# Expert outputs of a mixture of experts added straight into the output rows, with a weight ring of three

## The chip, the cores and the metric

The kernel runs on one core of one Trainium2 chip. A core has five engines with instruction streams of their own: TensorE (PE, matrix products; its weight loads are shown apart as PEld), VectorE (DVE), ScalarE (ACT), GpSimd (POOL) and SyncE (SP), which here only issues transfers. They wait for each other with semaphores. Sixteen DMA engines move data between the memory of the chip and the on-chip buffer; transfers are issued from SP, ACT (hardware queues) or POOL (the software queue, the one that does indirect transfers). Matrix products write to PSUM, and an engine copies the result out. The metric is the device time in microseconds of one execution, lower is better.

## The reference

One decoder layer for 512 prompt tokens and 8 sample tokens (520 rows of 1024 values, f32). The change lies in the last part, a mixture of experts in which each token goes to one group and inside it to two experts:

```python
def hier_moe(x, g_ffn, w_group, w_router, w_gate, w_up, w_down):
    h = rmsnorm(x, g_ffn).reshape(b * t, d)
    g_logits = jnp.dot(h, w_group)                      # 4 groups
    g_sel = jnp.argmax(g_logits, axis=-1)
    g_w = softmax(g_logits) at g_sel
    e_in_group = jnp.dot(h, w_router) of group g_sel    # 8 experts each
    top_val, top_idx = lax.top_k(e_in_group, 2)
    top_w = jax.nn.softmax(top_val, axis=-1) * g_w
    ...
    def add_expert(acc, params):
        wg, wu, wd, c = params                          # (1024,512) (1024,512) (512,1024)
        act = jax.nn.silu(h @ wg) * (h @ wu)
        return acc + (act @ wd) * c[:, None], None
y = x + hier_moe(x, ...)
```

There are 32 experts. Each has three weight matrices of 2 MB in f32, so all weights together are 192 MB, and every one of them is read.

## The kernel before

The layer up to the mixture (projections, two attentions, output projections) takes the first 794 us and is untouched but for one line of clearing. The rest has three blocks, one after the other. Between blocks all engines meet at a barrier.

**`route`** normalises the rows (`hn`, stored in device memory as `token_rows`), computes the router's products, and finds on VectorE, in a chain of small dependent operations, which expert each token goes to and at which place. Each expert has a block of `CAP` = 64 rows; a token beyond 64 would go to one of 16 extra blocks (`NX`), which are run in a loop of their own, as often as needed (here no such round shows in the trace). From the places a small product on TensorE (`TB`, ten products with the one-hot tables `Rk` and `Bk`) makes `table[row, block]`, the token number of each place, or a number out of range for an empty place. SP meanwhile issues the weights of experts 0 and 1 into the two places of the ring `ew`, and behind them the stores of `hn`.

**`experts`** goes through the 32 experts with two sets of buffers (`j` = expert mod 2): two experts written out, then a hardware loop of 15 rounds with two experts each. For one expert:

- POOL copies a column of `table` to `idx` and gathers the rows to `xg` (an indirect transfer; empty places move nothing).
- PE turns `xg` (eight transposes to `TX`), DVE scales it into `xT`, PE forms the gate product `G` and the up product `U`. The 64 token rows fill only half the columns of the array, so each product is made in two halves of the hidden values side by side: half `h` takes the weight columns `HW*h` to `HW*h+255` and writes PSUM rows `64*h` on.
- ACT takes the sigmoid of `G`, DVE multiplies into `a`, PE turns `a` (`AT`), DVE copies it to `aT`, PE forms the down product `Y`.
- ACT copies `Y` to `y` and issues two stores of 128 KB into `expert_rows` (`eout`), all 64 rows, filled or not.
- SP waits in turn for the gate, up and down product of expert e-2 and issues the weights of expert e to the freed place.

In memory the gate and up weights of one partition are 8 rows side by side, 16 KB in one piece; the down weights of one partition are four rows of 4 KB that lie 512 KB apart (`"(j p) c -> p j c"`).

**`combine_experts`** gathers for each tile of 128 tokens its two expert rows (`yg`), DVE multiplies them with the weights `wt` and adds them to the residual `x`, and SP stores the tile to the output.

## Time and profile before

| | |
|---|---|
| median of 3 runs | 1392.73 us (1385.19 to 1395.62) |
| the profiled execution, own time | 1395.67 us |
| its span | 1393.4 us |
| before `route` | 0 to 794 us |
| `route` | 794 to 856 us |
| `experts` | 857 to 1366 us |
| `combine_experts` | 1368 to 1393 us |
| PE busy, share of the span | 1139.0 us, 82% |
| DVE busy | 506.3 us, 36% |
| memory read and written by DMA | 283.76 MB and 21.24 MB |

Read it by stage. The share of a busy engine is an average over blocks with different limits, and the change touches the last 600 us, where the DMA engines, PE and chains of small operations take turns as the limit.

### The profile page before, as it was taken

The numbers are of one execution on the slowest core, as the hardware profiler recorded it, in microseconds if no ns is written. First come the engines' busy times: TensorE is split into PE (matmuls) and PEld (weight loads), VectorE is DVE, ScalarE is ACT, GpSimd is POOL, SyncE is SP. The second block draws the span as 40 slices with busy tenths as digits, with TensorE's granted clock in tenths as the row PEclk, the third lists the DMA queues.
The fourth block names the chain that finished last, engine by engine and source line by source line (L and its number), as shares of the span: only waits on it lengthen the run. The fifth ranks groups of instructions, "written<-read, shape, count | busy, mean of one in ns | idle before, by whom it ended". The sixth has DMA issues, their size and how long they took to land. (4 is left out here: it accounts for less than half of the span.)

```text
span 1393.4 us, 16542 instructions
## 1 busy us (share of the span) xinstructions
PE 1139.0 (82%) x6089; PEld 604.4 (43%) x6089; DVE 506.3 (36%) x1187; ACT 179.6 (13%) x429; POOL 116.4 (8%) x161
## 2 busy tenths in 40 slices
PE   4989998895988899979999865888787878777771
PEld 3634444343555544423345354454444434444440
DVE  3426958974555256742113153111111111111113
ACT  2102221102444101101010100000000000000000
POOL 2012102200000000000010101000000000000003
PEclk9999999995577699989999955999999999999996
DMA  6332102103000345563540190999999999999995
GB/s 205 106 133 83 61 31 84 68 31 125 1 1 1 121 136 196 183 239 121 181 148 5 40 387 11 399 412 410 418 414 413 409 419 416 416 415 414 414 394 193
DMA packets 82263, 301.56 MB, mean 216 GB/s; under 512 B 17868, under 2 KB 17868, under 8 KB 74020
## 3 DMA queue, kind: packets, MB, share of 16 engines
q1 hardware_dynamic: 69108, 267.20, 49.3%
q0 software_dynamic: 7984, 25.30, 5.1%
q10 hardware_dynamic: 5120, 8.39, 1.7%
q8 instruction: 29, 0.48, 0.1%
q14 instruction: 22, 0.18, 0.0%
HBM read 283.76 MB, written 21.24 MB: 219 GB/s over the span
## 5 line engine op out<-in xcount | busy, mean ns | idle before, releaser
L344 PE MATMUL p_z<-m_w,m_xT 128*128 128x512 f32 (+2 forms) x528 | 214.6, 563 | 7.2 <-DMA m_w<-in_w_in 6.6
L1582 PE MATMUL e_Y<-x_ew,e_aT 128*64 128x512 f32 x512 | 128.8, 648 | 39.5 <-issue 21.3
L344 PEld LDWEIGHTS p_z<-m_w,m_xT 128*128 128x128 f32 (+1 forms) x528 | 95.1, 194 | 114.8 <-issue 107.7
L1567 PE MATMUL e_G<-x_ew,e_xT 128*64 128x256 f32 x1024 | 119.2, 386 | 29.2 <-DVE e_xT L1604 29.2
L1567 PE MATMUL e_U<-x_ew,e_xT 128*64 128x256 f32 x1024 | 117.0, 381 | 17.1 <-DMA x_ew<-in_w_up 17.1
L967 PE MATMUL g_ring<-m_w,m_xT 128*128 128x512 f32 x256 | 118.0, 615 | 0.0
L1567 PEld LDWEIGHTS e_G<-x_ew,e_xT 128*64 128x64 f32 x1024 | 78.0, 138 | 60.3 <-issue 18.9
L1567 PEld LDWEIGHTS e_U<-x_ew,e_xT 128*64 128x64 f32 x1024 | 74.4, 137 | 57.0 <-DMA x_ew<-in_w_up 24.9
L1582 PEld LDWEIGHTS e_Y<-x_ew,e_aT 128*64 128x64 f32 x512 | 42.4, 147 | 105.2 <-issue 81.0
L1604 DVE TENSOR_TENSOR e_xT<-e_TX,x_gffn 128x512 f32<-128x512 f32 x32 | 22.1, 692 | 179.6 <-PE e_TX L1558 179.6
L967 PEld LDWEIGHTS g_ring<-m_w,m_xT 128*128 128x128 f32 x256 | 49.0, 197 | 63.3 <-issue 62.1
L1607 DVE TENSOR_TENSOR e_den<-e_sig,e_G 128x256 f32<-128x256 f32 x32 | 13.5, 421 | 138.4 <-ACT e_sig L1590 138.4
L1594 ACT COPY e_y<-e_Y 128x512 f32<-128x512 f32 x32 | 18.7, 585 | 321.0 <-PE e_Y L1582 321.0
L1612 DVE TENSOR_TENSOR e_a<-e_den,e_U 128x256 f32<-128x256 f32 x32 | 13.5, 421 | 106.6 <-PE e_U L1567 106.6
L724 ACT ACTIVATE a_prob<-a_masked,a_nb 128x128 f32<-128x128 f32 (+3 forms) x64 | 35.9, 561 | 78.4 <-DVE a_nb L806 78.2
L1182 DVE TENSOR_TENSOR g_prod<-g_page_k,g_B 128x512 f32<-128x512 f32 x64 | 41.0, 680 | 6.5 <-PE g_B L1004 4.0
L681 PE MATMUL a_S<-t_Tkd,t_Tqd 64*128 64x128 f32 (+3 forms) x64 | 30.8, 749 | 12.9 <-DVE a_nb L806 9.2
L1621 POOL COPY e_idx<-x_table 64x1 int32 (+1 forms) x32 | 5.7, 178 | 397.3 <-PE e_TX L1558 397.3
L660 PEld LDWEIGHTS a_O<-t_vvs,a_pT 128*128 128x128 f32 x160 | 34.3, 304 | 0.1
L461 POOL TENSOR_TENSOR p_rs<-p_rs,k_c 128x8 f32<-128x8 f32 (+1 forms) x20 | 33.6, 1680 | 1.7
L967 PE MATMUL g_ring<-g_wod,m_oTd 128*128 128x512 f32 x64 | 30.9, 628 | 3.4 <-DMA g_wos<-in_w_o_dsa 3.4
L660 PE MATMUL a_O<-t_vvs,a_pT 128*128 128x64 f32 x160 | 33.6, 369 | 0.0
(332 smaller groups left out, 1277.4 us busy)
## 6 DMA issues: line engine op xcount, KB each, us to landing
x_ew<-in_w_gate SPq DMA_DIRECT2D x32, 2048.0 KB, 26.9
x_ew<-in_w_up SPq DMA_DIRECT2D x32, 2048.0 KB
x_ew<-in_w_down SPq DMA_DIRECT2D x32, 2048.0 KB, 27.8
m_w<-in_w_in SPq DMA_DIRECT2D x9, 2048.0 KB, 7.7
g_page_k<-in_cache_diff_k SPq DMA_DIRECT2D x32, 256.0 KB, 2.7
g_page_k<-in_cache_dsa_k SPq DMA_DIRECT2D x32, 256.0 KB, 2.8
g_page_v<-in_cache_diff_v SPq DMA_DIRECT2D x32, 256.0 KB, 4.2
g_page_v<-in_cache_dsa_v SPq DMA_DIRECT2D x32, 256.0 KB, 3.1
```

The lines of the kernel that those rows point to most:

```text
L344: last = nc.tensor.matmul(z[u % 3][0:p, 0:WIDTH[k]], s.xT[:, j, 128 * i:128 * i + p], s.w[:, c % 2, j, 0:WIDTH[k]], start=j == 0, stop=j = ...
L461: nc.gpsimd.tensor_tensor(rs[0:p, n % 2, :], rs[0:p, n % 2, :], s.c[0:p, C_MH:C_MH + H], ALU.pow).then_inc(rs_ready, 1)
L660: last = nc.tensor.matmul(O[g % 2][:, w * h:w * h + w], pT[:, q % 2, 128 * b:128 * b + 128], s.v[KQV[kind][2]][:, b, w * h:w * h + w], sta ...
L681: nc.tensor.matmul(S[n % 3][:, 0:128 * (t + 1)], s.T[kq][r:r + 64, h // 2, 128 * t:128 * t + 128], s.T[kk][r:r + 64, h // 2, 0:128 * (t + ...
L724: nc.scalar.activation(prob[:, n % 4, 0:w], masked[:, n % 3, 0:w], ACT.Exp, bias=nb[:, n:n + 1], scale=DH ** -0.5, accum_out=sums[:, n:n + ...
L967: last = nc.tensor.matmul(bank[:], x[:, j, 128 * i:128 * i + 128], w[:, j, :], start=j == 0, stop=j == steps - 1)
L1182: v.tensor_tensor(prods[m % 2][:], page["k"][:, m % PLACES, :], B[nq % 2][:], ALU.mult).then_inc(k_used, 1)
L1567: last = nc.tensor.matmul(bank[CAP * h:CAP * h + CAP, 0:HW], xT[:, j, b, :], s.ew[n][:, j, b, HW * h:HW * h + HW], start=b == 0, stop=b == ...
L1582: last = nc.tensor.matmul(Y[j][CAP * h:CAP * h + CAP, :], aT[:, b % 2, CAP * (b // 2):CAP * (b // 2) + CAP], s.ew[2][:, j, b, W * h:W * h ...
L1594: nc.scalar.copy(y[j][:], Y[j][:]).then_inc(y_out, 1)
L1604: v.tensor_tensor(xT[:, j], TX[:], bcast(s.gffn[:], CAP, 2), ALU.mult).then_inc(xT_out, 1)
L1607: v.tensor_tensor(den[:], sig[:], G[j][:, 0:HW], ALU.mult).then_inc(chain, 1)
```

## The change

- The combination block is gone, and with it `expert_rows`. In `route` ACT stores the residual `x` to the output before the experts run. In `experts` ACT multiplies each row with its weight while it copies `Y` (`share[:, e]`, from a second table product `WB` in `route`), and POOL adds the 128 half rows of 512 values into the output with indirect transfers whose operation is an addition in memory: one for the prompt rows (`to_p`), one for the sample rows (`to_s`), each skipping the places that are not its own. POOL waits until both adds of the expert before have landed before it issues new ones.
- The ring of weights has three places (`DEPTH`), three experts are issued in `route`, and the 32 experts are written out with no hardware loop. Stores of `hn` move from SP to ACT.
- PE turns the rows of the next expert between the up product and the turning of `a`.
- The down weights of a partition are now four adjacent rows, 16 KB in one piece. So that the hidden values match, half `h` of the gate and up products takes of each four weight columns the two from `2*h` on (`own`), and `a` is turned by every second column (`every`).

```diff
-            nc.gpsimd.memset(zero, 0.0).then_inc(zeroed, 1)
-            rest = s.eout[NE * CAP:NBLK * CAP, :].rearrange("(p r) (q c) -> p (r q) c", p=128, c=256)
-            pool.dma_start(rest, bcast(zero, rest.shape[1], 1)).then_inc(rest_zeroed, 16)
...
 def route(nc, io, s):
-            for e in range(2):
+            for e in range(DEPTH):
                 for n, wt in enumerate(("w_gate", "w_up", "w_down")):
                     sp.dma_start(s.ew[n][:, e], s.expert(io[wt], e, n)).then_inc(s.ew_in[n][e], 16)
-            for i, p in enumerate(ROWS):
-                sp.wait_ge(hn_ready, i + 1)
-                sp.dma_start(s.rows[128 * i:128 * i + p, :], hn[0:p, i].rearrange("p j q -> p (j q)")).then_inc(stored[i % 2], 16)
...
+            for i, p in enumerate(ROWS):
+                act.wait_ge(hn_ready, i + 1)
+                act.dma_start(s.rows[128 * i:128 * i + p, :], hn[0:p, i].rearrange("p j q -> p (j q)")).then_inc(stored, 16)
+            for i, p in enumerate(ROWS):
+                dst = io["y_p"][128 * i:128 * i + p, :] if i < NT else io["y_s"]
+                act.dma_start(dst, s.x[0:p, i, :]).then_inc(stored, 16)
...
-                last = nc.tensor.matmul(TB[:], Rk[0:p, m, :], Bk[0:p, m, :], start=m == 0, stop=m == 2 * TILES - 1)
+                last = nc.tensor.matmul(TB[:], Rk[0:p, m, :], Wk[0:p, m, :], start=m == 0, stop=m == 2 * TILES - 1)
+            last.then_inc(tabled, 1)
+            pe.wait_ge(tab_in, 2)
+            for m in range(2 * TILES):
+                p = ROWS[m % TILES]
+                last = nc.tensor.matmul(WB[:], Rk[0:p, m, :], Bk[0:p, m, :], start=m == 0, stop=m == 2 * TILES - 1)
...
+            link(v.tensor_tensor(Bk, Bk, bcast(wt[:].rearrange("p k t -> p (k t)"), NBLK, 2), ALU.mult))
+            link(v.scalar_tensor_tensor(unfilled[:], TB[:], -1.0, unfilled[:], ALU.add, ALU.add))
+            link(v.tensor_scalar(unfilled[:], unfilled[:], 2.0, half[:], ALU.mult, ALU.add))
+            link(v.tensor_copy(s.to_p[:], unfilled[:]))
+            link(v.tensor_scalar(early[:], unfilled[:], 2.0 * SEQ, NO_ROW, ALU.is_lt, ALU.mult))
+            link(v.scalar_tensor_tensor(s.to_s[:], unfilled[:], -2.0 * SEQ, early[:], ALU.add, ALU.add))
+            dve.wait_ge(tabled, 2)
+            link(v.tensor_copy(s.share[:], WB[:]))
...
 def experts(nc, io, s):
+        own = lambda ap, h: ap.rearrange("p (q f) -> p q f", f=4)[:, :, 2 * h:2 * h + 2]
+        pair = lambda ap: ap.rearrange("p (q f) -> p q f", f=2)
+        every = lambda ap, f: ap.rearrange("p (q f) -> p f q", f=2)[:, f, :]
+        def up_product(bank, j, n, r):
+            for b in range(KD):
+                for h in range(2):
+                    last = nc.tensor.matmul(pair(bank[CAP * h:CAP * h + CAP, 0:HW]), xT[:, j, b, :], own(s.ew[n][:, r, b, :], h),
+                                            start=b == 0, stop=b == KD - 1)
...
+            for e in range(DEPTH, NE):
+                for n, (wt, done) in enumerate(zip(EXPERT_WEIGHTS, (g_done, u_done, d_done))):
+                    sp.wait_ge(done, e - DEPTH + 1)
+                    sp.dma_start(s.ew[n][:, e % DEPTH], s.expert(io[wt], e, n)).then_inc(s.ew_in[n][e % DEPTH], 16)
...
+                act.wait_ge(d_done, e + 1)
+                if e >= 2:
+                    act.wait_ge(y_added, 32 * (e - 1))
+                nc.scalar.activation(y[j][:], Y[j][:], ACT.Copy, scale=s.share[:, e:e + 1]).then_inc(y_out, 1)
...
+            def add_rows(n, to_p, to_s):
+                nc.gpsimd.indirect_dma_start(out=s.halves_p, out_offset=bass.IndirectOffsetOnAxis(ap=to_p, axis=0),
+                                             in_=y[n][:], in_offset=None, bounds_check=2 * SEQ - 1, oob_is_err=False,
+                                             compute_op=ALU.add).then_inc(y_added, 16)
+                nc.gpsimd.indirect_dma_start(out=s.halves_s, out_offset=bass.IndirectOffsetOnAxis(ap=to_s, axis=0),
+                                             in_=y[n][:], in_offset=None, bounds_check=2 * NS - 1, oob_is_err=False,
+                                             compute_op=ALU.add).then_inc(y_added, 16)
...
-def combine_experts(nc, io, s):
...
-    s.expert = lambda ap, e, n: ap[0, e].rearrange("(p j) c -> p j c", j=KD) if n < 2 else ap[0, e].rearrange("(j p) c -> p j c", p=128)
+    s.expert = lambda ap, e, n: ap[0, e].rearrange("(p j) c -> p j c", j=KD if n < 2 else 4)
```

TensorE, first experts, before (`e_TX` is the turning of the rows, `e_AT` that of `a`):

```order
L1558 MATMUL e_TX<-k_c,e_xg 128x64 x8
L1567 MATMUL e_G<-x_ew,e_xT 64x256 x16
L1567 MATMUL e_U<-x_ew,e_xT 64x256 x16
L1574 MATMUL e_AT<-k_c,e_a 128x128 x2
L1582 MATMUL e_Y<-x_ew,e_aT 64x512 x8
L1558 MATMUL e_TX<-k_c,e_xg 128x64 x8
L1567 MATMUL e_G<-x_ew,e_xT 64x256 x16
```

The same place after:

```order
L1577 MATMUL e_TX<-k_c,e_xg 128x64 x8
L1583 MATMUL e_G<-x_ew,e_xT 64x256 x16
L1583 MATMUL e_U<-x_ew,e_xT 64x256 x16
L1577 MATMUL e_TX<-k_c,e_xg 128x64 x8
L1589 MATMUL e_AT<-k_c,e_a 128x128 x2
L1595 MATMUL e_Y<-x_ew,e_aT 64x512 x8
L1583 MATMUL e_G<-x_ew,e_xT 64x256 x16
```

The turning of the next expert's rows stands ahead of `e_AT` instead of behind `e_Y`, so the gate product follows the down product directly.

GpSimd, the loop body of two experts before:

```order
L1621 ISA [waits e_x_turned]
L1621 COPY e_idx<-x_table 64x1
L1622 REGISTER_ALU
L1624 DMA e_xg<-token_rows,e_idx 64x1024 [waits e_idx_ready]
L1621 ISA [waits e_x_turned]
```

GpSimd after, in the middle of the experts:

```order
L1739 DMA e_xg<-token_rows,x_table 64x1024 [waits e_x_turned]
L1744 DMA out_y_p<-e_y,x_to_p 1024x512 [waits e_y_added,e_y_out]
L1747 DMA out_y_s<-e_y,x_to_s 16x512
L1739 DMA e_xg<-token_rows,x_table 64x1024 [waits e_x_turned]
L1744 DMA out_y_p<-e_y,x_to_p 1024x512 [waits e_y_added,e_y_out]
```

Each gather now stands behind the two adds of an earlier expert, and these wait for the adds before them.

## Rows read from the trace of the kernel before

**Rows 1.** The page: mean GB/s in 40 slices of 34.8 us

```profile
GB/s 205 106 133 83 61 31 84 68 31 125 1 1 1 121 136 196 183 239 121 181 148 5 40 387 11 399 412 410 418 414 413 409 419 416 416 415 414 414 394 193
```

**Rows 2.** Busy time by stretch; last three columns: PE clock, DMA share, GB/s

```profile
core 0: us, PE busy (x) PEld busy (x) DVE busy (x) ACT busy (x) POOL busy (x), PEclk, DMA share, GB/s
835.00:870.00 35.00, 18.06 (x104) 15.22 (x106) 14.19 (x44) 1.33 (x2) 5.46 (x8) 0.53 0.04 11
870.00:1357.00 487.00, 384.79 (x2808) 213.33 (x2806) 61.13 (x125) 30.35 (x63) 33.01 (x58) 0.98 1.01 412
1357.00:1364.40 7.40, 5.92 (x36) 2.40 (x32) 0.85 (x2) 0.04 (x1) 0.00 (x0) 1.00 0.09 36
```

**Rows 3.** Timeline of one expert on PE: start, us, what, idle before

```profile
1105.43 0.71 PE L1558 MATMUL e_TX<-k_c,e_xg 64*128 64x64 f32 x8
...
1107.20 3.67 PE L1567 MATMUL e_G<-x_ew,e_xT 128*64 128x256 f32 x32 [1.06 <-DVE e_xT L1604]
...
1111.78 3.67 PE L1567 MATMUL e_U<-x_ew,e_xT 128*64 128x256 f32 x32 [0.91 <-DMA x_ew<-in_w_up]
...
1116.03 0.44 PE L1574 MATMUL e_AT<-k_c,e_a 128*128 128x128 f32 x2 [0.58 <-DVE e_a L1612]
...
1118.57 3.65 PE L1582 MATMUL e_Y<-x_ew,e_aT 128*64 128x512 f32 x16 [2.10 <-issue]
```

**Rows 4.** Timeline of the last 35 us: last down product, end of the combination

```profile
1360.67 3.65 PE L1582 MATMUL e_Y<-x_ew,e_aT 128*64 128x512 f32 x16 [0.82 <-DVE e_aT L1616]
1364.36 0.58 ACT L1594 COPY e_y<-e_Y 128x512 f32<-128x512 f32 x1 [9.95 <-PE e_Y L1582]
...
1391.24 0.34 SPq L1784 DMA_DIRECT2D out_y_s<-k_x  x1
```

**Rows 5.** Timeline of the route and the first expert

```profile
838.04 6.59 PE L1415 MATMUL r_RK<-r_C,k_c 128*128 128x32 f32 x30
...
849.83 0.82 DVE L1500 TENSOR_TENSOR r_Rk<-k_c,r_rk 128x640 f32<-128x640 f32 x1
...
852.34 2.86 PE L1422 MATMUL r_TB<-r_Bk,r_Rk 128*64 128x48 f32 x20 [7.71 <-DVEq L1505]
...
855.91 0.20 DVE L1523 SCALAR_TENSOR_TENSOR x_table<-r_TB,r_unfilled 64x48 int32<-64x48 f32 x1
...
870.11 0.38 SPq L1632 DMA_DIRECT2D x_ew<-in_w_gate  x1
```

**Rows 6.** Stretches of 5 us of the first weight load, columns as Rows 2

```profile
803.00:808.00 5.00, 5.00 (x24) 4.62 (x23) 1.36 (x2) 0.00 (x0) 0.00 (x0) 0.50 1.00 429
808.00:813.00 5.00, 4.22 (x21) 4.20 (x21) 1.78 (x2) 0.00 (x0) 0.00 (x0) 0.50 0.97 398
...
818.00:823.00 5.00, 4.22 (x20) 3.81 (x20) 2.46 (x3) 0.00 (x0) 0.00 (x0) 0.50 1.00 419
823.00:828.00 5.00, 3.84 (x33) 3.49 (x32) 1.11 (x6) 0.00 (x0) 0.00 (x0) 0.50 0.98 374
```

**Rows 7.** DMA packets from 803 to 808 us, then from 808 to 813

```profile
DMA packets 147, 2.15 MB, mean 429 GB/s; under 512 B 16, under 2 KB 16, under 8 KB 16
...
DMA packets 493, 1.99 MB, mean 398 GB/s; under 512 B 16, under 2 KB 16, under 8 KB 490
```

**Rows 8.** DMA queues from 870 to 1360 us: packets, MB, share of 16 engines

```profile
q1 hardware_dynamic: 24479, 188.75, 93.5%
q10 hardware_dynamic: 4960, 8.13, 4.5%
q0 software_dynamic: 2320, 3.90, 2.5%
```

**Rows 9.** The gather (two rows), and landing of the expert_rows stores (third)

```profile
L1624 POOL DMA_INDIRECT e_xg<-token_rows,e_idx x32: 957/961/1128, 859.6 to 1318.7; - x32
...
DMA to landing us min/median/max: 2.9/8.0/8.9
...
DMA to landing us min/median/max: 2.3/6.9/11.0
```

**Rows 10.** The ten microseconds after the clearing store was issued, columns as Rows 2

```profile
30.00:40.00 10.00, 10.00 (x22) 4.33 (x22) 2.14 (x4) 0.00 (x0) 0.09 (x1) 1.00 0.96 366
```

More of the change, by code:

```diff
@@ L36 @@
 NO_ROW = 65536.0
+DEPTH = 3
 EPS = 1e-6
@@ L1580, in pe_block, with turn_hidden, down_product @@
+        def turn_hidden():
+            for f in range(2):
+                last = nc.tensor.transpose(AT[:, f, :], every(a[:], f), s.ident[:])
+            return last
+        def down_product(bank, r):
             for b in range(4):
                 for h in range(2):
-                    last = nc.tensor.matmul(Y[j][CAP * h:CAP * h + CAP, :], aT[:, b % 2, CAP * (b // 2):CAP * (b // 2) + CAP],
-                                            s.ew[2][:, j, b, W * h:W * h + W], start=b == 0, stop=b == 3)
@@ L1584, in pe_block @@
-            last.then_inc(d_done, 1)
-        def act_block(act, e, it, j, first):
-            act.wait_ge(g_done, e + 1)
-            if not (first and j == 0):
-                act.wait_ge(a_ready, e)
-            nc.scalar.activation(sig[:], G[j][:, 0:HW], ACT.Sigmoid).then_inc(gated, 1)
-            act.wait_ge(d_done, e + 1)
-            if not first:
-                act.wait_ge(y_stored[j], it * 32)
-            nc.scalar.copy(y[j][:], Y[j][:]).then_inc(y_out, 1)
-            act.wait_ge(y_out, e + 1)
-            for h in range(2):
-                act.dma_start(s.out_rows(e)[:, W * h:W * h + W], y[j][CAP * h:CAP * h + CAP, :]).then_inc(y_stored[j], 16)
@@ L1628, in sp_block @@
-        def sp_block(sp, e, it, j, first):
-            for n, (wt, done) in enumerate((("w_gate", g_done), ("w_up", u_done), ("w_down", d_done))):
-                sp.wait_ge(done, e - 1)
-                sp.dma_start(s.ew[n][:, j], s.expert(io[wt], e, n)).then_inc(s.ew_in[n][j], 16)
-        def run(eng, step, peel=True):
-            if peel:
-                for j in range(2):
-                    step(eng, j, 0, j, True)
-            with eng.Fori(1, NE // 2) as it:
-                for j in range(2):
-                    step(eng, it * 2 + j, it, j, False)
+                    last = nc.tensor.matmul(bank[CAP * h:CAP * h + CAP, :], aT[:, b % 2, CAP * (b // 2):CAP * (b // 2) + CAP],
+                                            s.ew[2][:, r, b, W * h:W * h + W], start=b == 0, stop=b == 3)
@@ L1643, in extra @@
+            return last
         def extra(eng, step):
@@ L1742, in step @@
+            gather(0, s.table[:, 0:1])
+            gather(1, s.table[:, 1:2])
+            for e in range(NE):
+                if e + 2 < NE:
+                    pool.wait_ge(x_turned, e + 1)
+                    gather(e % 2, s.table[:, e + 2:e + 3])
+                pool.wait_ge(y_out, e + 1)
+                if e:
+                    pool.wait_ge(y_added, 32 * e)
+                add_rows(e % 2, s.to_p[:, e:e + 1], s.to_s[:, e:e + 1])
+            pool.wait_ge(y_added, 32 * NE)
             def step(pool, b):
```

276 lines of the change are left out of this document (122 added, 154 removed).

## The prediction

> **What bounds the kernel now.** I read the page's row of transferred GB/s first [rows 1]. In its 24th slice the DMA engines run at 387 GB/s, in the 25th at 11, and from the 26th on at about 400 to 419 until the end of the experts. So the weights start in `route`, stop because the ring of two is full, and once the experts run they never stop again. The stretches put numbers on it [rows 2]: 35 us at a DMA share of 0.04 (835 to 870), then 487 us at a share of 1.01 and 412 GB/s, then 7.4 us in which PE finishes. The combination takes the remaining 29 us, 1364.4 to 1393.4.
>
> The 487 us are 30 experts, since two were loaded ahead: **16.23 us an expert**. Is PE also near its limit? From one expert's turning of rows to the gate product takes PE 1.77 us, the gate and up products 3.67 us each, the turning 0.44 us and the down product 3.65 us [rows 3]. Add to the 1.77, 7.34, 0.44 and 3.65 about 1.0 us for the two small DVE steps around the turning, and PE could pass an expert in some 14.2 us. The up product's 0.91 us of idle time is put down to its weights, and the 2.10 us before the down product has no releaser in the trace. With the DMA engines at share 1.01 I take both for waiting on weights. The stage is bound by transfers with PE 2 us behind. The rest is serial: `route`'s chain before the first product, and the combination.
>
> **The change, part by part.** All sums are made against the profiled execution: span 1393.4 us, own time 1395.67 us, 2.9 us over the median of 1392.73.
>
> *The clearing store* of 4 MB goes. While it runs PE is busy 10.00 of 10 us [rows 10], so it was hidden: 0.
>
> *The route gets longer.* The one-hot table `Rk` is made twice as wide, one more operation of 0.82 us. The table product's stationary operand goes from 64 to 128 columns: it cost 2.86 us for 20 instructions, 0.143 each; the rank product with 128 columns cost 6.59 us for 30, 0.22 each [rows 5]. So `TB` takes about 4.4 us and ends near 852.34 + 0.8 + 4.4 = 857.6. The new product `WB` needs the weighted `Bk` (one more operation of some 0.7 us on DVE, hidden behind `TB`) and runs behind it for another 4.4 us, to 862. The five new small DVE operations of 0.2 us (the size of the row for `x_table`) lie beside `WB`; the last copy does not. `route` ends near 862.1 instead of 856.1: **+6 us**. Bounds: +3, if the two products keep 0.143 us each (0.8 + 2.86 and a little less than 0), and +9, if PE's issue is slower than both rows.
>
> *The stores of `hn` and `x`* (2.1 MB each) move to or start on ACT's queue. Three experts and both stores are 18.9 + 4.3 = 23.1 MB, at 412 GB/s 56 us from 798, so 855. That is before 862: hidden, with 7 us of cover. Should it not hold, its excess delays the barrier by so much.
>
> *The ring of three.* The weights restart when expert 0's gate product is done, at 870.11 [rows 5], now at about 876 with the longer route. From there 29 experts are to be loaded, not 30. So the third load falls into the 35 us in which the DMA engines stood still. At the old rate that is worth 16.2 us, less the 6 us of `route`. This third place also lets PE run one expert further ahead.
>
> *The size of pieces.* During the first load, stretches with gate and up weights (147 packets for 2.15 MB, all but 16 of them over 8 KB) ran at 429 and 419 GB/s. Those with down weights (493 packets for 1.99 MB, nearly all of 4 KB) ran at 398 and 374 [rows 6, 7]. 2.1 MB take 4.95 us at 424 and 5.43 us at 386. The second of the low stretches also holds small router work and the start of the row stores, so I take **0.35 us an expert**, bounds 0.1 and 0.55. The Trainium skill's page "DMA: Bandwidth & Descriptors" (Specifications) puts the transfer size from which full rate is reached at 512 B. By that rule 4 KB and 16 KB are alike, this term is zero, and the sum comes out 10 us later. The rows differ by 7 to 12%, so I follow them, but keep zero inside the range.
>
> *Stores against adds.* The stores to `expert_rows` took 4.5% of 16 engines over 490 us for 8.13 MB [rows 8]: 22 us in all, 2.7 us a MB, 0.71 us an expert. They go. The adds move only filled places: 1040 token rows of 4 KB are 4.26 MB, 0.133 MB an expert. No row shows an add in memory. Its lower bound is a plain store of so much, 0.133 x 2.7 = 0.36 us. If the read of the destination costs like a gather (2.5% of 490 us for 3.90 MB, 3.1 us a MB [rows 8]), 0.42 us come on top, 0.78 us. I take 0.6, nearer to the upper, because both reads must happen and only their overlap is open.
>
> **New period**: 16.23 - 0.35 - 0.71 + 0.6 = **15.77 us**; bounds 15.3 and 16.2. PE with the rows turned early saves the 1.1 us before the gate product, and needs about 13 us (7.34 + 3.65 + 0.71 + 0.44 + about 0.9 for the DVE steps). That stays below, so PE's reordering is worth nothing by itself.
>
> *The new wait on POOL.* The adds of one expert wait until those of the expert before have landed; behind them on POOL stands the gather for an expert two further on. Gathers land 8.0 us (median) after issue under the same load, the stores 6.9 us, 11.0 at most, and one indirect transfer costs POOL 0.96 us [rows 9]. Two issues and a landing of 8 to 11 us make 10 to 13.5 us, below 15.77: hidden. The cover is 2 to 5 us.
>
> *The end.* Loads end at 876 + 29 x 15.77 = 1333.3. The up weights have landed some 5 us before, so the last up product is over by then. After `a` and its turning the down product starts close to 1333.5 and ends at 1337.3: 4 us behind the loads instead of 7.4 [rows 2, 4]. Then come ACT's copy (0.7 us with its wait), two issues on POOL (2.3 us) and one landing on idle DMA engines. The shortest landings were 2.9 us for a gather and 2.3 for a store [rows 9]; I take 3.2. The span ends at about 1344 with half a microsecond of closing. So the tail behind the last product is 6.7 us instead of 29.0 [rows 4]: **-22 us**.
>
> **Sum**: +6 (route), -16.2 (one expert fewer), -13.3 (29 x 0.46), -3.4 (end of PE), -22.3 (tail) = -49. That is 1395.67 - 49 = 1346.5 of its own time, or 1343.5 from the median. I predict 1345 us.
>
> **The rivals.**
>
> *1. The period does not move.* The pieces of 4 KB cost nothing after all or the adds cost what the stores did; 16.2 us stay. The overlap in [rows 6] between 398 and 419 speaks for it. That gives 1345 + 29 x 0.46 = 1358 us, still faster. With adds at twice the gather's price (another 0.4 us an expert) it is 1370.
>
> *2. Adds hold up the weight queue (slower than before).* An add must read its destination before it writes. Each expert has 65 packets of 2 KB, 4 for each DMA engine. If an engine serves nothing else while it waits for the read, each packet costs a round trip: the shortest landing, 2.3 us [rows 9], bounds it. 4 x 2.3 = 9.2 us an expert gives 1345 + 29 x 9 = about 1600 us; a fourth of that, 0.6 us a packet, gives 1345 + 29 x 2.3 = 1412 us. The point from which it decides is 49 us over 29 experts, 1.7 us an expert or 0.42 us a packet. The landing of the adds also feeds POOL's wait: above 13.4 us the period is landing plus 2.3 us, and above 15.1 us the gain is gone. Against it: the three queues now share the same engines, and q1 gets 93.5% beside them. The Trainium skill's "DMA: Bandwidth & Descriptors" (section on back-pressure in remote DMA) says that stalled writes stall the other queues of the engine as well. That rule is on this rival's side, and no row here shows a stalled write.
>
> *3. The gate and up products slow down (slower than before).* Their moving operand now takes two values, skips two, takes two. No product in the trace reads so. At half speed they cost 7.34 us more, PE needs 20.3 us an expert and becomes the bound: about 1510 us. The point is a product of 5.8 us instead of 3.67. The Trainium skill's "SBUF — State Buffer" (Door 1: The DMA port swizzle) asks for two reads in a line for full speed, and here each line gives exactly two f32 values. By that rule nothing slows. No row here tests it.
>
> *4. The change doesn't prefetch.* If the third load does not finish before the experts start, for want of room beside the stores, part of the 16 us is lost: up to 1361 us.
>
> **How the numbers follow.** Forecast (period 15.3 to 16.0) 0.62; rivals 1 and 4 together 0.20, all faster by over 1%; rival 2 with a loss of less than the gain 0.05; rival 2 in full 0.08; rival 3 0.05. A measurement of this kernel can tell about 1% (14 us) from no change. Faster by over 1%: 0.62 + 0.20 and a little of the mild case, 0.83; within 1%: 0.04; slower: 0.13. The low end is the period of 15.3 with a route of +3 and no more, 1345 - 14 = 1331; the high end takes in rival 1 with the dear adds, 1372.
>
> **What would show it.** In the profile after: the DMA share near 1 from about 876 on without a break and the last weights near 1333; gate products issued 15.8 us apart; packets over 8 KB for down weights too; gate and up products still 3.67 us; adds landing in 8 to 11 us, and POOL waiting for the down product and not for the adds; the last product followed by under 8 us. I am wrong if the weight queue's rate falls below 400 GB/s in the stage (adds), if PE idles nowhere for weights (products), or if the DMA engines stand still again after 880.

## The result, and the profile after

The changed kernel takes **1402.3 us** (median of 20 runs, 1390.6 to 1408.2), the kernel before 1393.8 us on the same chip. The ratio is 1.0064, 95% interval 1.0045 to 1.0084: 9 us slower, where 1345 us was forecast. The profiled execution has a span of 1406.1 us and an own time of 1407.9 us.

The page of the kernel after (40 slices of 35.2 us) answers to [rows 1], and its chain of waits names a new end:

```profile
GB/s 163 78 87 76 68 31 83 61 32 122 1 1 1 141 159 198 239 178 134 139 130 1 153 428 126 409 409 392 390 382 395 401 393 395 397 366 399 397 261 14
...
DMA out_y_s<-e_y,x_to_s 27%; DMA e_xg<-token_rows,x_table 1%; PE e_Y L1595 1%; PE e_G L1583 1%; POOL out_y_p L1744 1%; PE e_U L1583 1%; PE e_TX L1577 0%; POOL out_y_s L1747 0%; PE e_AT L1589 0%; POOL e_xg L1736 0%; DVE e_aT L1716 0%; ACT e_y L1682 0%; POOLq L1747 0%; POOLq L1744 0%; DVE e_xT L1701 0%
```

The weights still flow until the 38th slice, but at 366 to 401 GB/s in most slices instead of 409 to 419. The end of the span now hangs for 27% of it on the landing of adds. The stretches (columns as [rows 2]):

```profile
835.00:870.00 35.00, 19.22 (x88) 17.72 (x90) 16.02 (x47) 1.28 (x1) 4.83 (x5) 0.50 0.47 196
...
900.00:1300.00 400.00, 320.73 (x2124) 161.67 (x2121) 44.75 (x96) 24.62 (x47) 98.78 (x72) 0.88 1.00 393
1300.00:1357.00 57.00, 47.02 (x340) 24.71 (x336) 6.44 (x14) 4.28 (x8) 12.34 (x9) 0.91 1.01 397
1357.00:1395.00 38.00, 31.09 (x198) 15.18 (x198) 4.15 (x9) 2.83 (x5) 10.34 (x7) 0.87 0.15 29
```

The third load does fill the gap before the experts (share 0.47 from 835 to 870 against 0.04 in [rows 2]). But the last weights land near 1357 and PE then works another 37 us, on three experts whose weights lie ready. PE no longer follows the weights; something else holds it. The timeline of PE shows what (start, us, what, idle before):

```profile
1111.67 3.80 PE L1583 MATMUL e_G<-x_ew,e_xT 128*64 128x256 f32 x32
1115.30 3.79 PE L1583 MATMUL e_U<-x_ew,e_xT 128*64 128x256 f32 x32
1124.69 1.12 PE L1577 MATMUL e_TX<-k_c,e_xg 64*128 64x64 f32 x8 [5.59 <-DMA e_xg<-token_rows,x_table]
1125.73 0.70 PE L1589 MATMUL e_AT<-k_c,e_a 128*128 128x128 f32 x2
1126.95 6.16 PE L1595 MATMUL e_Y<-x_ew,e_aT 128*64 128x512 f32 x16 [0.52 <-DVE e_aT L1716]
```

Up product, then 5.6 us of waiting for gathered rows, then a down product at 6.16 us instead of the 3.65 of [rows 3]: PE stood still for those 5.6 us, and the granted clock is 0.50, the lower of its two levels (1.2 GHz), from 1122 to 1132 us, before it is back at 1.00 (mean 0.88 in the stage, 0.97 before over the same 400 us). POOL waits for landings all the same, so this slower work of PE lies inside its wait. And the gather is late because of POOL:

```profile
1104.32 1.56 POOL L1744 DMA_INDIRECT out_y_p<-e_y,x_to_p  x1 [11.56 <-DMA out_y_s<-e_y,x_to_s]
1106.19 1.56 POOL L1747 DMA_INDIRECT out_y_s<-e_y,x_to_s  x1 [0.30 <-issue]
1108.05 0.99 POOL L1739 DMA_INDIRECT e_xg<-token_rows,x_table  x1 [0.30 <-issue]
1122.33 1.56 POOL L1744 DMA_INDIRECT out_y_p<-e_y,x_to_p  x1 [13.29 <-DMA out_y_s<-e_y,x_to_s]
```

POOL waits, issues the two adds and a gather, and waits again for the adds to land. From the first such add at 885.04 to the 29th at 1357.79 it makes 28 rounds, **16.88 us each**. The waits of POOL from 900 to 1340 us (total, times, longest) and the rows of the sample adds say the same:

```profile
POOL out_y_p L1744 <- DMA out_y_s<-e_y,x_to_s: 316.1, 26, 14.2
```

```profile
L1747 POOL DMA_INDIRECT out_y_s<-e_y,x_to_s x32: 1553/1557/1575, 887.0 to 1397.2; - x32
...
DMA to landing us min/median/max: 2.7/14.3/16.3
```

Of 27 waits in this stretch 26 end with a landing, and none with a down product. An issue of an add costs POOL 1.56 us (0.96 for a gather, [rows 9]), and the second add lands 14.3 us after its issue (median), where gathers took 8.0 [rows 9]. The queues from 900 to 1340 us (packets, MB, share), against [rows 8]:

```profile
q1 hardware_dynamic: 11369, 165.57, 92.5%
q0 software_dynamic: 9654, 7.04, 7.5%
```

The software queue carries 371 packets an expert (9654 over 26 rounds), before 77 (2320 over 30 experts, [rows 8]). Filled places alone are some 98 an expert, 33 rows gathered and 65 half rows added. From 900 to 1300 us 4452 packets of this queue have 8 bytes, 186 for each of 24 experts, and the two adds of an expert skip 191 places (256 less 65). So in an add a skipped place makes a small packet too; e2 below bears this out.

The end (answers to [rows 4]):

```profile
1390.21 3.65 PE L1595 MATMUL e_Y<-x_ew,e_aT 128*64 128x512 f32 x16 [0.52 <-DVE e_aT L1716]
...
1395.38 1.55 POOL L1744 DMA_INDIRECT out_y_p<-e_y,x_to_p  x1 [9.10 <-ACT e_y L1682]
1397.24 1.55 POOL L1747 DMA_INDIRECT out_y_s<-e_y,x_to_s  x1 [0.30 <-issue]
```

From the end of the last product (1393.9) to the end of the span are 12.2 us, 29.0 before. The last sample add lands 2.8 us after its issue, at 1400.0; in the 6.1 us behind that no engine works and no packet moves (columns as [rows 2]):

```profile
DMA to landing us min/median/max: 2.8/2.8/2.8
...
1400.00:1406.00 6.00, 0.00 (x0) 0.00 (x0) 0.00 (x0) 0.00 (x0) 0.00 (x0) 0.50 0.00 0
```

### The profile page after: what moved, and what is told of

The parts are those of the page before. It is cut to its first block and busy times, and to the rows that moved or that the text cites. A ratio compares the mean times of both kernels' runs of the same rounds, so it can differ in the third digit from the quotient of the medians.

```text
span 1406.1 us, 15962 instructions
## 1 busy us (share of the span) xinstructions
PE 1180.0 (84%) x6109; PEld 609.7 (43%) x6109; DVE 493.2 (35%) x1186; ACT 182.8 (13%) x429; POOL 198.8 (14%) x181
## 5 line engine op out<-in xcount | busy, mean ns | idle before, releaser
L1595 PE MATMUL e_Y<-x_ew,e_aT 128*64 128x512 f32 x512 | 153.1, 753 | 16.6 <-DVE e_aT L1716 16.6
L1583 PE MATMUL e_U<-x_ew,e_xT 128*64 128x256 f32 x1024 | 121.3, 387 | 0.0
L1707 DVE TENSOR_TENSOR e_den<-e_sig,e_G 128x256 f32<-128x256 f32 x32 | 13.5, 421 | 265.5 <-ACT e_sig L1678 265.5
L1744 POOL DMA_INDIRECT out_y_p<-e_y,x_to_p x32 | 50.0, 1563 | 381.5 <-DMA out_y_s<-e_y,x_to_s 329.5
L1577 PE MATMUL e_TX<-k_c,e_xg 64*128 64x64 f32 x256 | 27.1, 259 | 85.6 <-DMA e_xg<-token_rows,x_table 85.6
L1583 PEld LDWEIGHTS e_G<-x_ew,e_xT 128*64 128x64 f32 x1024 | 72.5, 136 | 58.8 <-issue 19.6
L1682 ACT ACTIVATE e_y<-e_Y,x_share 128x512 f32<-128x512 f32 x32 | 22.0, 687 | 394.7 <-PE e_Y L1595 332.4
L1577 PEld LDWEIGHTS e_TX<-k_c,e_xg 64*128 64x128 f32 x256 | 22.2, 165 | 99.6 <-DMA e_xg<-token_rows,x_table 94.7
L1747 POOL DMA_INDIRECT out_y_s<-e_y,x_to_s x32 | 49.9, 1558 | 9.7 <-issue 9.7
L1716 DVE COPY e_aT<-e_AT 128x256 f32<-128x256 f32 x32 | 13.6, 424 | 105.6 <-PE e_AT L1589 105.6
L1712 DVE TENSOR_TENSOR e_a<-e_den,e_U 128x256 f32<-128x256 f32 x32 | 13.5, 421 | 91.1 <-PE e_U L1583 91.1
L1014 PE MATMUL g_O<-g_page_v,g_aZ 128*32 128x512 f32 x96 | 26.1, 642 | 11.2 <-DMA g_page_v<-in_cache_diff_v 10.3
## 6 DMA issues: line engine op xcount, KB each, us to landing
x_ew<-in_w_gate SPq DMA_DIRECT2D x32, 2048.0 KB, 12.2
```

What stands on the lines that cost most here:

```text
L1014: nc.tensor.matmul(acc[32 * n:32 * n + 32, :], aZ[:, n, b, :], page["v"][:, m % PLACES, :], start=b % group == 0, stop=n > 0 and b % group ...
L1577: last = nc.tensor.transpose(TX[:, b, :], xg[j][:, 128 * b:128 * b + 128], s.ident[0:CAP, 0:CAP])
L1583: last = nc.tensor.matmul(pair(bank[CAP * h:CAP * h + CAP, 0:HW]), xT[:, j, b, :], own(s.ew[n][:, r, b, :], h), start=b == 0, stop=b == KD ...
L1595: last = nc.tensor.matmul(bank[CAP * h:CAP * h + CAP, :], aT[:, b % 2, CAP * (b // 2):CAP * (b // 2) + CAP], s.ew[2][:, r, b, W * h:W * h ...
L1682: nc.scalar.activation(y[j][:], Y[j][:], ACT.Copy, scale=s.share[:, e:e + 1]).then_inc(y_out, 1)
L1744: nc.gpsimd.indirect_dma_start(out=s.halves_p, out_offset=bass.IndirectOffsetOnAxis(ap=to_p, axis=0), in_=y[n][:], in_offset=None, bounds_ ...
```

## The experiments

Three readings of the loss stood at the start. *The wait*: POOL's round of issue, landing and wait paces the experts. *The read*: an add is dear because it reads its destination. *Capacity*: adds and skipped places take the DMA engines from the weights. For the length of the landing there was a reading too: *turns*, each small packet waiting for a long weight packet on its DMA engine. All ratios are against the kernel before on the same chip, with their 95% interval. MB are what the weight queue moved from 900 to 1300 us; 6.29 MB an expert over that rate is the weights' period (before: 155.85 MB, 16.15 us; after: 150.56 MB, 16.71 us). Each of these figures comes from one profiled execution. The start of the experts moves between such executions (the first gather is issued at 846.1 us in e11 and at 866.4 in e2), so profiles are compared from there on, and whole times by their ratios.

**e1: plain stores in place of adds.** Rows overwrite each other, so the sum of the experts is left out.

```diff
-  in_=y[n][:], in_offset=None, ..., oob_is_err=False, compute_op=ALU.add).then_inc(y_added, 16)
+  in_=y[n][:], in_offset=None, ..., oob_is_err=False).then_inc(y_added, 16)
```

> The changed kernel with the addition taken out of its 64 indirect output transfers: they overwrite the half rows instead (so the output rows hold one expert's part only), with the same packets, issues and waits. Theory A (turns): every packet of the software queue, one for a skipped place too, waits for a weight packet of 16 KB on its engine, 0.64 us at 412 GB/s over 16 engines; 18 packets an engine and expert make the landing. Then the landing of the sample transfer stays at 12 to 14 us (14.3 in the changed kernel) and the time within 1% of the changed kernel, 1390 to 1405 us. Theory B (the read before the write is the cost): landing falls under 9 us, POOL waits for the down product instead, and the time falls to 1350 to 1370 us.

Measured: 1364.0 us, ratio 0.9795 (0.9736 to 0.9854). 155.75 MB, as before the change. The timing of the sample transfers:

```profile
L1746 POOL DMA_INDIRECT out_y_s<-e_y,x_to_s x32: 983/992/1008, 881.9 to 1350.2; - x32
DMA to landing us min/median/max: 2.1/10.1/11.4
```

The landing lies between what the two theories wanted (12 to 14 us, and under 9). The addition costs 0.57 us at each issue and 4 us at the landing (10.1 against 14.3), and its absence is worth 38 us. POOL now waits for ACT's copy of the down product, 26 times between 900 and 1340, and for a landing three times. The software queue's packets are fewer too: 250 an expert against 359 (4507 and 6456 over the 18 gathers from 1000 to 1300 us), with a little more data: plain stores make 97 packets of 8 bytes an expert instead of 186. So this run takes away the read, packets and most of the wait at once, and doesn't tell them apart.

**e2: no adds to the sample rows** (their expert part is left out).

```diff
-  nc.gpsimd.indirect_dma_start(out=s.halves_s, ..., compute_op=ALU.add).then_inc(y_added, 16)
-  pool.wait_ge(y_added, 32 * e)
+  pool.wait_ge(y_added, 16 * e)
```

> The changed kernel without the adds into the sample rows (the 8 sample rows keep their residual, the experts' part is left out). Half of the places and one of two issues go. Both theories expect a landing of the prompt add of 9 to 11 us (10.9 before), so 1.6 + 11 + 0.7 = 13.3 us around POOL's loop, under the 16.2 us of the weights. If the wait on POOL is what sets the stage, the time falls to 1360 to 1380 us and PE waits for weights again. If the DMA engines themselves are the limit (theory C: small packets cost them rate), it falls by less than 10 us, since the weights' bytes are the same.

Measured: 1370.1 us, ratio 0.9831 (0.9787 to 0.9876); the prompt adds land in 11.4 us, 153.47 MB. From 1000 to 1300 us the software queue moves 4078 packets instead of 6456 (132 fewer an expert) at 4.91 MB instead of 4.84: nearly every place of the removed transfer is skipped, and each of its 128 places was a packet. The packets of 8 bytes are 64 an expert now, and the prompt add skips some 63 of its 128 places. Yet the nearly empty transfer was worth 32 us. It was issued 1.86 us behind the prompt add and landed last: 14.3 us after its own issue, the prompt add 10.9 after its own.

**e3, e4: each weight matrix in four or two transfers**, with pieces of 4 or 8 KB.

```diff
+    m = dst.shape[1] // PARTS
+    for q in range(PARTS):
+        sp.dma_start(dst[:, m * q:m * q + m, :], src[:, m * q:m * q + m, :]).then_inc(s.ew_in[n][place], 16)
```

> The changed kernel with each weight matrix loaded by four transfers of 0.5 MB, so that each piece is 4 KB instead of 16 KB; nothing else. Theory A: a packet of the software queue now waits 0.16 us for its turn instead of 0.64, the sample add lands in 5 to 7 us, POOL waits for the down product, and the time falls to 1350 to 1375 us. Theory B and theory C: landing and time stay, or the time rises by up to 10 us as pieces of 4 KB are slower by themselves.

> As e3 with two transfers a matrix, pieces of 8 KB. Theory A: a turn of 0.32 us, landing about 9 us, POOL's loop 12 to 13 us, below the period of the weights: the time as in e3 within 0.5%, 1350 to 1375 us. Theories B and C: no change against the changed kernel.

Measured: with 4 KB 1383.0 us, ratio 0.9929 (0.9907 to 0.9952), 8 us above the upper end of what was expected; with 8 KB **1372.8 us**, ratio 0.986 (0.9815 to 0.9904). The landing of the second add falls from 14.3 to 9.9 (8 KB) and 7.6 us (4 KB), the gather's from 16.0 to 10.0 and 6.8. In the 8 KB run POOL hardly waits for adds any more:

```profile
POOL out_y_p L1753 <- ACT e_y L1691: 267.5, 23, 15.5
POOL out_y_p L1753 <- DMA out_y_s<-e_y,x_to_s: 39.9, 5, 8.6
```

The adds are all there, so these 30 us are the wait and not what the adds take from the DMA engines. Between 8 and 4 KB the gain turns: the wait is already hidden, and the weights move 150.65 MB instead of 153.04.

**e5, e6: a ring of two**, with the pieces of the change and with 8 KB.

```diff
-DEPTH = 3
+DEPTH = 2
```

> The changed kernel with a ring of two (DEPTH = 2), adds and all else kept. If POOL's loop of two issues and a landing (16.9 us) sets the pace of the whole stage, the third place is worth nothing there, since PE never waits for weights: within 1% of the changed kernel, 1395 to 1412 us. If the weights are a limit beside it, the expert less to load shows: slower by 10 to 17 us.

> Ring of two with weight pieces of 8 KB (the version that ran in 1372.8 us, but for the ring). There the weights set the pace, so the third place should be worth the 16.2 us of one load: 1386 to 1392 us. If it is worth less than 8 us, the prediction's term for the ring is wrong.

Measured: 1402.1 us (ratio 1.0071, 1.0037 to 1.0105) and 1392.2 us (0.9979, 0.9952 to 1.0006). So in the changed kernel the third place is worth nothing. With 8 KB pieces it is worth 19 us by the medians (1392.2 to 1372.8), which come from two chips, and 17 by the ratios. In the changed kernel POOL waits 26 times for a landing with either ring; weights that lie ready earlier only wait longer.

**e7: stores to `expert_rows` and the combination as before**, with the rest of the change kept.

```diff
-                    act.wait_ge(y_added, 32 * (e - 1))
-                nc.scalar.activation(y[j][:], Y[j][:], ACT.Copy, scale=s.share[:, e:e + 1]).then_inc(y_out, 1)
+                    act.wait_ge(y_stored[j], 32 * (e // 2))
...
+def combine_experts(nc, io, s):
```

> The changed kernel with the adds undone: stores of 128 KB to expert_rows and the combination block as before, route without the second table product and without the store of x; kept are the ring of three, 16 KB pieces for all weights, the order on PE and the experts written out. Expected: route ends 5 us earlier than in the changed kernel, 29 experts at 15.9 to 16.2 us, 7 us for PE and 29 for the combination: 1362 to 1376 us. At 15.8 or less the prediction's term for the size of pieces (0.35 us) holds; at 16.2 it is zero.

Measured: 1387.1 us, ratio 0.9945 (0.992 to 0.997). That is 11 us above the upper end of what was expected. The combination takes its 29 us again, but the weights move only 152.56 MB, an expert in 16.49 us instead of 16.15. With the adds undone something still slows the weights; e9 to e15 look for it.

**e8: odd experts add to a second array**, so POOL waits for the adds of the expert before last. The odd experts' part is left out of the output; the adds and their packets are as many.

```diff
-                if e:
-                    pool.wait_ge(y_added, 32 * e)
+                if e >= 2:
+                    pool.wait_ge(y_in[e % 2], 32 * (e // 2))
```

> The changed kernel with 16 KB pieces, in which the adds of odd experts go to a second array in memory (their part is left out of the output), so that POOL waits only for the adds of the expert before the last; same packets, same bytes, and 2.1 MB more stored in route. If the wait for the adds of the expert before is what costs, the stage runs at the pace of the weights and the time falls to 1368 to 1385 us, though each landing stays at 14 us or more. If the adds cost by their packets on the DMA engines, it stays above 1392 us.

Measured: 1373.9 us, ratio 0.9843 (0.9801 to 0.9886), with 152.31 MB. All adds, the same pieces, the same issues of 1.56 us, and 28 us less: **without the wait the kernel is 1.6% faster than before, with it 0.6% slower**. Landings did not get shorter; the chain of waits has two of sample adds (start, us, what):

```profile
885.28 14.17 DMA out_y_s<-e_y,x_to_s
...
1031.04 17.73 DMA out_y_s<-e_y,x_to_s
```

POOL's waits of this run:

```profile
POOL other_p L1747 <- ACT e_y L1685: 149.6, 13, 13.8
POOL out_y_p L1747 <- ACT e_y L1685: 142.7, 14, 13.3
```

In e8 successive adds also go to different arrays; e4, which keeps one array and hides the wait in another way, gains as much, so this doesn't account for it. The 28 us are about half of the 57 that the changed kernel misses its forecast by. The rest is not the wait; the sections below put most of it on the weights' period and on the end.

**e9, e10, e11: the stores of e7** with down weights in four transfers (4 KB pieces as before), with a ring of two, and with both.

```diff
+    for q in range(4 if n == 2 else 1):
+        m = 1 if n == 2 else dst.shape[1]
+        sp.dma_start(dst[:, m * q:m * q + m, :], src[:, m * q:m * q + m, :]).then_inc(s.ew_in[n][place], 16)
```

> The kernel with expert_rows stores, the combination and a ring of three (1387.1 us), with the down weights issued in four transfers, so that their pieces are 4 KB as in the kernel before. Its weight queue moved 152.56 MB in 900:1300 (16.49 us an expert) against 155.85 MB before (16.15 us). Theory P (the 16 KB pieces of the down weights cost the lost rate): 155 MB or more, time 1376 to 1380. Theory R (the ring of three or the new order costs it, pieces are alike): 152 to 153.5 MB, time 1384 to 1390. The prediction on record (longer pieces are faster) wants under 151 MB and 1395 or more.

> The same kernel with expert_rows stores and 16 KB pieces, with a ring of two. The ring of three should be worth the third load, which falls into the standstill of the DMA engines in the route: 13 to 17 us, so 1400 to 1404 here, with the same 152 to 153 MB in 900:1300. If the ring of three is what lowers the rate in the stage (theory R), the rate goes back to 155 MB or more and the time is 1390 to 1396.

> Ring of two and down weights in 4 KB pieces, stores and combination: the kernel before but for the order on PE, the experts written out, the operand with steps and stores of hn from ACT. Theory P or R alone: the rate of before, 155 to 156 MB, and its time within 4 us (1390 to 1398). If the rate stays at 152 to 153.5 MB and the time at 1400 or more, neither pieces nor ring is the cause, and the cost lies in the order on PE or in the experts written out.

| | us | ratio (interval) | MB | GB/s |
|---|---|---|---|---|
| e7 ring 3, down 16 KB | 1387.1 | 0.9945 (0.992 to 0.997) | 152.56 | 408 |
| e9 ring 3, down 4 KB | 1388.8 | 0.9975 (0.9949 to 1.0001) | 151.00 | 404 |
| e10 ring 2, down 16 KB | 1399.9 | 1.0044 (1.002 to 1.0068) | 153.31 | 409 |
| e11 ring 2, down 4 KB | 1402.4 | 1.0083 (1.0047 to 1.0118) | 151.46 | 404 |

The ring of three is worth 12.8 and 13.6 us here, near the forecast. Pieces of 16 KB for the down weights move 1% more, 0.17 and 0.20 us an expert. Neither pieces nor ring lowers the rate.

**e12: e10 with the order of the down weights of before** (and the plain operand of the products). **e15: e12 with the next rows turned behind the down product**, as before; the edit shown is that of e15.

```diff
-                if e + 1 < NE:
-                    rows(e + 1)
                 pe.wait_ge(a_ready, e + 1)
...
                 down_product(Y[j], r).then_inc(d_done, 1)
+                if e + 1 < NE:
+                    rows(e + 1)
```

> Stores and combination, ring of two, and now the down weights in the order of before (rows 512 KB apart, 4 KB pieces), with the plain operand of the gate and up products and the plain turning of the hidden values. What is left of the change is the order on PE, the experts written out, and the stores of hn from ACT. Theory M (the new order of the down weights in memory costs the rate): 155 MB or more in 900:1300 and 1390 to 1396 us. Theory U (order on PE or the experts written out): 151 to 153.5 MB and 1399 to 1403 us, as without this edit.

> The run with stores, ring of two and the old order of the down weights (1405.2 us, 151.9 MB in 900:1300), with the rows of the next expert turned behind the down product, as in the kernel before. What is left is the experts written out without a loop. If the early turning of rows costs the rate (the gate product and the release of its weights come at another moment): 155 MB or more and 1390 to 1396 us. If the experts written out cost it: 151 to 152.5 MB and 1401 to 1407 us.

Measured: e12 1405.2 us (ratio 1.0101, 1.0068 to 1.0134) with 151.87 MB; the order in memory is not the cause. e15 1395.2 us (1.0021, 0.9991 to 1.005) with 155.55 MB, all but the 155.85 of before. The weight queue of e12 and of e15, 900 to 1300 us:

```profile
q1 hardware_dynamic: 19674, 151.87, 94.2%
```

```profile
q1 hardware_dynamic: 19992, 155.55, 94.0%
```

So it is the early turning of the next rows, which by itself made the weights 2.4% slower with a ring of two: 0.4 us an expert and 10 us in all (from the first gather to the end of the span the two profiles take 544.0 and 534.1 us). The queue is busy for the same share in both; each packet takes longer. Why the moment at which PE turns the rows matters to the transfers, no run showed.

**e13, e14: the changed kernel and e4, with down weights as before** (order and 4 KB pieces). **e16: e4 with the rows turned behind the down product.**

```diff
-    s.expert = lambda ap, e, n: ap[0, e].rearrange("(p j) c -> p j c", j=KD if n < 2 else 4)
+    s.expert = lambda ap, e, n: ap[0, e].rearrange("(p j) c -> p j c", j=KD) if n < 2 else ap[0, e].rearrange("(j p) c -> p j c", p=128)
```

> The changed kernel (1402.3 us) with only the order and pieces of the down weights as before; gate and up weights keep pieces of 16 KB. By the prediction on record this gives 10 us away. By the turns of the software queue behind weight packets, a third of the packets are now 4 KB: the adds land in 11 to 13 us instead of 14.3, POOL's loop takes 14.5 to 16 us and no longer bounds, and with theory M the rate rises: 1368 to 1380 us. If landing stays at 14 us, 1400 or more.

> The fastest kernel with adds so far (two transfers for each matrix, 8 KB pieces, 1372.8 us) with the order of the down weights as before, 4 KB pieces for them. Theory M: the rate rises from 153.0 to 154.5 MB or more, 0.2 us an expert or more, 1362 to 1368 us. Theory U: no change, 1370 to 1376 us, or a few us more for the shorter pieces.

> The fastest kernel with adds so far (two transfers for each matrix, 8 KB pieces, ring of three, 1372.8 us) with the rows of the next expert turned behind the down product. PE then needs the 1.1 us for DVE's copy of the turned rows again, about 14.3 us an expert, which stays below the weights' 16.4. If the order costs rate: 154 MB or more and 1364 to 1369 us; if not, 1370 to 1376 us.

Measured: e13 1391.9 us (1.0005, 0.9971 to 1.0038); e14 1383.5 us (0.9942, 0.9914 to 0.997), 11 us *more* than e4; e16 1377.5 us (0.9892, 0.9852 to 0.9932) with 152.72 MB, which can't be told from e4: the intervals overlap, and from the first gather on the two profiles take 516.7 and 516.8 us. So what e15 showed for stores and a ring of two doesn't carry over to adds and a ring of three. In e13 the gathers land sooner (13.5 us against 16.0), but the adds as late as in the changed kernel, against what was expected of it:

```profile
L1747 POOL DMA_INDIRECT out_y_s<-e_y,x_to_s x32: 1553/1557/1575, 886.1 to 1387.5; - x32
DMA to landing us min/median/max: 2.7/14.2/15.1
```

Its rounds are 17.1 us from the sixth on (16.9 in the changed kernel), but the first five of the stage take 11.1 to 15.9 us instead of 13.9 to 18.7; there its 10 us come from. Why, stays open.

**e17: two transfers a matrix as in e4, but each of 64 partitions with 16 KB pieces.**

```diff
-        sp.dma_start(dst[:, m * q:m * q + m, :], src[:, m * q:m * q + m, :])...
+        sp.dma_start(dst[64 * q:64 * q + 64], src[64 * q:64 * q + 64])...
```

> The changed kernel (1402.3 us, adds to the sample rows land 14.3 us after their issue) with each weight matrix in two transfers of 64 partitions each, so two transfers as in the run with 8 KB pieces (1372.8 us, 9.9 us), but pieces of 16 KB. If the length of the pieces sets the landing (turns behind long packets): it stays at 13.5 to 15 us and the time at 1398 to 1406 us. If the number of transfers does: 9 to 11 us and 1370 to 1378 us.

Measured: 1742.8 us (1674.7 to 1766.0, four runs), which no theory had. The weights run at 56% of their speed (84.46 MB against 150.56), and the adds land in 24.5 us:

```profile
900.00:1300.00 400.00, 209.56 (x1336) 106.02 (x1334) 27.61 (x60) 16.05 (x30) 61.80 (x45) 0.74 1.02 221
...
q1 hardware_dynamic: 6447, 84.46, 95.9%
...
L1755 POOL DMA_INDIRECT out_y_s<-e_y,x_to_s x32: 1553/1557/1575, 903.5 to 1724.5; - x32
...
DMA to landing us min/median/max: 3.0/24.5/26.2
```

It is no clean test of the length of pieces, since the rate changed with it, yet it bears on the turns. The time of one large weight packet (share of the weight queue, times 16 engines, times 400 us, by its packets of 4 KB and more) against the landing of the second add:

| | large packets | us each | landing, us |
|---|---|---|---|
| e3, 4 KB | 39293 | 0.155 | 7.6 |
| e4, 8 KB | 18704 | 0.321 | 9.9 |
| after, 16 KB | 9210 | 0.643 | 14.3 |
| e17, 16 KB of 64 partitions | 5169 | 1.19 | 24.5 |

The first three lie on a line of 5.5 us and 13.8 packets; the fourth would be 21.9 by it. The number of transfers is two in e4 and in e17, with 9.9 and 24.5 us, so it doesn't set the landing; the landing follows the time of a weight packet.

The packets show the turns themselves. While both adds of an expert are under way, the software queue starts about one packet for each packet of weights, whatever those take. Counted in the trace (weight packets of 4 KB and more):

| | us | software queue | weight packets |
|---|---|---|---|
| e3, 4 KB | 1107 to 1111 | 259 | 339 |
| e4, 8 KB | 1114 to 1119 | 199 | 225 |
| after, 16 KB | 1109 to 1115 | 151 | 140 |
| e13, 16 and 4 KB | 1112 to 1118 | 195 | 196 |
| e17, 16 KB of 64 partitions | 1103 to 1115 | 149 | 158 |

More than half of the software queue's packets have 8 bytes and take 9 ns; what they cost is their turn. So a nearly empty transfer could matter in e2. The line above is not a law, though: by the mean time of all its weight packets (0.29 us) e13 would land in 9.5 us, and it takes 14.2.

## Why the prediction was wrong

**"The new wait on POOL" is the step that failed**: "two issues and a landing of 8 to 11 us make 10 to 13.5 us, below 15.77: hidden". (The terms given make 9.9 to 12.9, and 10.3 to 13.3 with the 2.3 us that rival 2 adds to a landing.) The landing was 14.3 us. The forecast of it was taken from gathers and stores, which do no addition and don't stand behind another indirect transfer of their own queue. e1 puts 4 us on the addition and its packets, e2 shows that the second, nearly empty transfer counts in full, e3, e4 and the packet counts that the small packets take turns with the weight packets. Two issues were priced at 0.96 us each and are 1.56. The round is 16.9 us, and e8 and e4, which hide it in different ways, are 28 and 30 us faster.

The step had a second fault: the yardstick. The round was compared with the weights' 15.77 us. But with three experts loaded ahead, 32 experts have to pass POOL from the first add (885) to the last one of the forecast (1338.7): 31 rounds in 454 us, **14.6 us each**. The measured 31 (885.04 to 1395.38) took 16.46 us on average, 57 us more in all. This fault is the larger one: with the prediction's own rule (landing plus 2.3 us, 29 times) the measured landing of 14.3 us would have given 16.6 us a round and 1369 us in all. So the cover was not "2 to 5 us" but about 1 to 4.5, and the break-even landing was about 12 us (14.6 less the 2.6 that separate round and landing), not the 13.4 of rival 2. That rival held the mechanism ("the landing of the adds also feeds POOL's wait"), with 0.13 for it and the delay of the weights together. What it was mainly about, adds that hold up the weight queue itself, was small: 3% less rate than before (150.56 against 155.85 MB).

**"New period" 15.77 us failed as well**, by less. With the wait hidden (e4) it was 16.44, which is 29 x 0.67 = 19 us. Its terms:

- *The size of pieces*, -0.35: right in sign for the down weights at 4 KB against 16 KB, but 0.17 to 0.20 (e9, e11), and for the whole kernel swamped by what long pieces do to the landing. The rows of the first load overstated it; that the low stretches also held other traffic may be why, and no run tested it. (Rival 1 spoke of an overlap between 398 and 419 GB/s in them. There is none: the high stretches have 419 and 429, the low ones 374 and 398.) The Trainium skill's "DMA: Bandwidth & Descriptors" (Specifications), with full rate from 512 B, was the better guide here: pieces of 4 KB against 8 KB cost 1.6% of the rate (e3, e4), not nothing but little.
- *Stores against adds*, -0.71 + 0.6: the software queue moves 0.27 MB an expert, 4.84 over 18 (adds and gathers, 0.13 each, as reckoned), but "the adds move only filled places" left out the packets of skipped places. e1 against e8, both with pieces of 16 KB and with little waiting for landings, gives 0.36 us an expert (16.16 and 16.52) for the addition and its packets; e1 against e4, with 8 KB, 0.28 (16.16 and 16.44).
- *PE's order*, "worth nothing by itself": it cost 0.4 us an expert in the kernel with stores and a ring of two (e12, e15).

**The ring of three** was priced right (16.2 forecast, 12.8 and 13.6 in e7 to e11, 17 to 19 in e4 and e6), but is worth nothing as long as POOL's round binds (e5).

**The route** came out right: +6 forecast, +4.5 measured.

```profile
850.58 4.99 PE L1424 MATMUL r_TB<-r_shared 128*128 128x48 f32 x20 [8.36 <-DVEq L1514]
...
855.50 4.99 PE L1429 MATMUL r_WB<-r_shared 128*128 128x48 f32 x20
...
874.58 0.33 SPq L1613 DMA_DIRECT2D x_ew<-in_w_gate  x1
```

The gate weights of the fourth expert are issued at 874.58 (870.11 before, [rows 5]; 876 forecast). Each product cost 0.25 us an instruction, a little above 0.22. The stores were hidden: no transfer runs from 855 to 860.

**Rival 3** is refuted: gate and up products take 3.80 us instead of 3.67 (a matmul 388 ns against 379), 3% and not double. The Trainium skill's "SBUF — State Buffer" (Door 1: The DMA port swizzle) had led to nothing slowing, and the trace nearly agrees. **The end** was -22 us and became -16.8 (29.0 to 12.2). Copy, issues and landing take 6.2 us together, as assumed (the landing 2.8, 3.2 assumed). What was too small is the "half a microsecond of closing": 6.1 us pass from the last landing to the end of the span. What they are, no trace shows.

Sum, in spans: 1344 forecast, 57 for the rounds from the first add to the last, 5 for the end: 1406. Of the 57, e8 and e4 take away 28 to 30; the longer period of the weights explains 19 of the others, and some 10 stay without an account.

## What to carry to other kernels

A wait for the landing of one's own transfers is a loop of its own; add up its issues and its landing, and compare it with the time per round that the forecast end asks for after prefetching, not with the period of the stream that bounds now. A landing under load must be priced for the same kind of transfer in the same queue, with the skipped places of adds counted as packets and each packet taking turns with one of the other queue's. Here shorter pieces of the heavy stream (8 KB) shortened every small transfer beside it: the changed kernel with that one edit is the fastest that keeps the whole computation, 1372.8 us, 1.4% below the kernel before.

## What the hardware showed unexpectedly

- An indirect transfer with an addition costs GpSimd 1.56 us to issue, a plain one 1.0 us, and it lands about 4 us later under load.
- In an indirect transfer with an addition a skipped place still makes a packet, of 8 bytes: the nearly empty adds to the sample rows were 132 packets an expert (e2). In the gathers of the kernel before a skipped place makes none: their queue has 812 packets of 4 KB and 1200 of 4 bytes from 900 to 1300 us, and none of 8.
- While adds are under way, the software queue starts about one packet for each weight packet (151 and 140 in 6 us with 16 KB, 199 and 225 in 5 us with 8 KB), so its small packets land the later the longer a weight packet takes.
- Loads to 64 partitions at a time left the engines at 221 GB/s, loads to 128 at 393 (e17 and the changed kernel, all queues), with the DMA engines shown as fully busy in both (share 1.02 and 1.00).
- Turning the next rows earlier on TensorE lowered the rate of the weights by 2.4% in one kernel (155.55 to 151.87 MB in 400 us), with the DMA share unchanged.
